# Expert rows without a token skipped, outputs scattered by assignment, all low halves on VectorE

## The reference

```
# hierarchical_moe: 4 groups of 8 experts, top group, then 2 experts inside it; N = 1024 tokens
gate = p_g * softmax(top_v);  expert = g_idx * 8 + top_i          # (N, 2): 2048 assignments
dest_sorted = pstarts[e_sorted] + arange(2N) - starts[e_sorted]   # slots: blocks of 128, one expert each
buf_tok = zeros(P).at[dest_sorted].set(tok_flat[order])           # a slot without a token holds token 0
out_buf = map(lambda tok, e: (silu(xt[tok] @ w1[e]) * (xt[tok] @ w3[e])) @ w2[e], blocks)
y = einsum('nk,nkd->nd', gate, out_buf[dest])
# then x = x + y, and an RMS norm with a gain
```

## Time and profile before

| | us |
|---|---|
| median of 3 runs | 2969.07 |
| profiled execution | 2971.06 |
| its span, first to last instruction | 2969.2 |
| mean granted TensorE clock | 0.947 |

### The profile page before, as it was taken

The page is one execution under the profiler, slowest core; times in us unless marked ns, Lnnn a source line. Parts: engine busy times, 40 slices in busy tenths (PEclk is TensorE's granted clock), DMA queues, the critical chain, the costliest instruction groups (busy, mean ns, idle before and its releaser), DMA issues. The chain is left out here.

```text
span 2969.2 us, 31008 instructions
## 1 busy us (share of the span) xinstructions
PE 2599.6 (88%) x12104; PEld 2095.0 (71%) x12104; DVE 1203.7 (41%) x1637; ACT 1177.7 (40%) x1701; POOL 1036.8 (35%) x613
## 2 busy tenths in 40 slices
PE   6999978879899999899978799938977999999991
PEld 5888856668778878688867577835766777777770
DVE  4530027754122212223436522005135666666654
ACT  3212227754232122123214422214215777777762
POOL 3212203323212122313204532354103667666662
PEclk9999989999999999999979999979987999999995
DMA  4432145532211130422144333371444999999976
GB/s 152 145 119 92 53 102 138 130 93 86 85 50 43 64 107 29 118 75 92 57 136 141 107 121 110 132 289 57 148 186 178 374 375 374 384 374 373 375 293 248
DMA packets 173025, 490.35 MB, mean 165 GB/s; under 512 B 13936, under 2 KB 81552, under 8 KB 160208
## 3 DMA queue, kind: packets, MB, share of 16 engines
q1 hardware_dynamic: 117856, 382.62, 36.4%
q10 hardware_dynamic: 40080, 52.97, 4.9%
q0 software_dynamic: 14944, 52.78, 4.8%
HBM read 389.23 MB, written 99.09 MB: 164 GB/s over the span
## 5 line engine op out<-in xcount | busy, mean ns | idle before, releaser
L2524 ACT ACTIVATE ex_w_hi<-ex_w 128x2048 fp32r<-128x2048 f32 x198 | 378.7, 1916 | 169.8 <-DMA ex_w<-w 102.6
L2584 DVE TENSOR_TENSOR ex_w_lo<-ex_w,ex_w_hi 128x2048 fp32r<-128x2048 f32 x132 | 345.3, 2654 | 197.8 <-ACT ex_w_hi L2524 197.8
L227 POOL TENSOR_TENSOR p_w_lo<-w_raw,p_w_hi 128x512 fp32r<-128x512 f32 (+1 forms) x154 | 198.1, 1316 | 621.5 <-ACT p_w_hi L247 620.1
L2408 POOL TENSOR_TENSOR ex_w_lo<-ex_w,ex_w_hi 128x2048 fp32r<-128x2048 f32 x66 | 340.5, 5183 | 205.2 <-ACT ex_w_hi L2524 205.2
L227 POOL TENSOR_TENSOR p_w_lo_rest<-w_raw,p_w_hi_rest 128x512 fp32r<-128x512 f32 x94 | 123.1, 1343 | 275.0 <-ACT p_w_hi_rest L247 275.0
L366 PE MATMUL o_ps<-o_w_hi,o_m_hi 128*128 128x512 f32 x384 | 154.9, 403 | 19.8 <-POOL split_cols L1028 19.8
L368 PE MATMUL o_ps<-o_w_hi,split_cols 128*128 128x512 f32 x384 | 153.1, 399 | 0.0
L367 PE MATMUL o_ps<-o_w_lo,o_m_hi 128*128 128x512 f32 x384 | 152.9, 398 | 0.0
L366 PE MATMUL ex_pa<-ex_w_hi,ex_xT_hi 128*128 128x512 f32 x264 | 108.2, 410 | 31.4 <-issue 28.7
L1028 POOL TENSOR_TENSOR split_cols<-plain_cols,o_m_hi 128x1024 fp32r<-128x1024 f32 x24 | 57.3, 2391 | 214.0 <-ACT o_m_hi L1078 214.0
L366 PE MATMUL p_ps<-p_w_hi,hT_hi 128*128 128x512 f32 (+1 forms) x320 | 121.6, 380 | 2.6 <-PEq L279 2.6
(11 more groups left out here) (429 smaller groups left out, 6607.2 us busy)
## 6 DMA issues: line engine op xcount, KB each, us to landing
ex_w<-w SPq DMA_DIRECT2D x99, 2048.0 KB, 15.4
w_raw<-w_in SPq DMA_DIRECT2D x42, 1024.0 KB, 5.2
y_slots<-ex_y ACTq DMA_DIRECT2D x33, 512.0 KB, 12.0
y_slots<-xp_zero POOLq DMA_DIRECT2D x32, 512.0 KB, 16.8
att_k<-k_columns SPq DMA_DIRECT2D x48, 256.0 KB, 7.8
x_rows<-o_x SPq DMA_DIRECT2D x24, 512.0 KB, 2.6
w_raw<-w_out SPq DMA_DIRECT2D x8, 1024.0 KB, 9.7
qk_columns<-qk_y ACTq DMA_DIRECT2D x16, 512.0 KB, 2.6
```

Source lines behind the costliest of these rows:

```text
L227: emit(self.lo(n)[:, 0:w], self.half(n // (KC // 2), w)[:, n % (KC // 2), :], self.hi(n)[:, 0:w].bitcast(F32), ALU.subtract).then_inc(self ...
L2408: nc.gpsimd.tensor_tensor(w_lo[:, n % RING, :], raw_half(n), w_hi[:, n % RING, :].bitcast(F32), ALU.subtract).then_inc(down_lo, 1)
L2524: nc.scalar.activation(w_hi[:, n % RING, :], raw_half(n), ACT.Copy).then_inc(hi_done, 1)
L2584: nc.vector.tensor_tensor(w_lo[:, n % RING, :], raw_half(n), w_hi[:, n % RING, :].bitcast(F32), ALU.subtract).then_inc(up_lo, 1)
```

## The change

- The zero fill in `memory_projections` is gone.
- The token table holds, per slot, k x 1024 + token + 1 instead of the token. `slot_row` is that less 1 where it is positive and a row past the end where it is zero; `slot_token` is the token, again past the end where there is none. Gathers have a bounds check that skips such rows. The gather buffer `xg` is cleared once by POOL during `route`, and now outlives that stage. `dest` is gone.
- y of a block is scattered by POOL into `y_rows` (2048 rows: assignment k of token t at k x 1024 + t), skipping empty slots, in place of ScalarE's store of all 128.
- `combine` loads these rows plainly, the first half on SP among the x tiles, the second on ScalarE's queue; its gathers are gone.
- The two low halves of w2 are made by VectorE, in the order of pieces; POOL makes none.

```
 # memory_projections, POOL
                 weights.take_los(pool)
-                nc.gpsimd.memset(zero[:, :], 0.0).then_inc(zero_ready, 1)
-                pool.wait_ge(zero_ready, 1)
-                for b in range(2 * S // P, NBLK):
-                    pool.dma_start(y_slots[b * P:(b + 1) * P, :], zero[:, :]).then_inc(cleared, 16)
-                pool.wait_ge(cleared, 16 * (NBLK - 2 * S // P))
 # route
+            @block.gpsimd
+            def _(pool):
+                nc.gpsimd.memset(xg[:, :, :], 0.0)
-                step(V.tensor_copy(dest[:, :, :], dest_f[:, :, :]))
                 for k in range(2):
-                    ins = V.tensor_tensor(d2[:, k * NT:(k + 1) * NT, :], d2[:, k * NT:(k + 1) * NT, :],
-                                          c.const("tokid").unsqueeze(2).to_broadcast([P, NT, NBLK]), ALU.mult)
+                    half = d2[:, k * NT:(k + 1) * NT, :]
+                    ins = V.scalar_tensor_tensor(half, c.const("tokid").unsqueeze(2).to_broadcast([P, NT, NBLK]),
+                                                 float(k * S + 1), half, ALU.add, ALU.mult)
-                V.memset(slot_token[:, NBLK:], 0)
-                step(V.tensor_copy(slot_token[:, 0:NBLK], pt[:, 0:NBLK]))
+                step(V.tensor_scalar(d2[:, 0, :], pt[:, 0:NBLK], 0.5, float(NOWHERE), ALU.is_lt, ALU.mult))
+                step(V.scalar_tensor_tensor(d2[:, 1, :], pt[:, 0:NBLK], -1.0, d2[:, 0, :], ALU.add, ALU.add))
+                V.tensor_copy(slot_row[:, :], d2[:, 1, :])
+                step(V.tensor_scalar(d2[:, 2, :], d2[:, 1, :], float(S), -float(S), ALU.is_ge, ALU.mult))
+                step(V.tensor_tensor(slot_token[:, :], d2[:, 1, :], d2[:, 2, :], ALU.add))
 # experts, POOL (in gather: bounds_check=S - 1, oob_is_err=False)
-                def take_lo(n):
-                    m, b, half = pieces[n]
-                    pool.wait_ge(hi_done, n + 1)
-                    nc.gpsimd.tensor_tensor(w_lo[:, n % RING, :], raw_half(n), w_hi[:, n % RING, :].bitcast(F32),
-                                            ALU.subtract).then_inc(down_lo, 1)
+                def scatter(b):
+                    pool.wait_ge(y_ready, b + 1)
+                    nc.gpsimd.indirect_dma_start(y_rows, bass.IndirectOffsetOnAxis(slot_row[:, b:b + 1].bitcast(U32), 0),
+                                                 y[:, b % 2, :], None, bounds_check=2 * S - 1, oob_is_err=False
+                                                 ).then_inc(y_out[b % 2], 16)
                 for n, m, b, half in steps():
-                    if n is not None and n + 3 in pieces and pieces[n + 3][0] == "w2":
-                        take_lo(n + 3)
                     if m == "turn_x" and b + 2 < NB:
                         gather(b + 2)
+                    if m == "w1" and half == 1 and b >= 2:
+                        scatter(b - 2)
+                scatter(NB - 2)
+                scatter(NB - 1)
 # experts, ScalarE, in store(b, n)
-                    act.wait_ge(y_ready, b + 1)
-                    act.dma_start(y_b[b], y[:, b % 2, :]).then_inc(y_out[b % 2], 16)
 # experts, VectorE
-                                            ALU.subtract).then_inc(up_lo, 1)
+                                            ALU.subtract).then_inc(down_lo if m == "w2" else up_lo, 1)
-                    if n is not None and n + 3 in pieces and pieces[n + 3][0] != "w2":
+                    if n is not None and n + 3 in pieces:
                         take_lo(n + 3)
 # combine, SP
                     sp.dma_start(x[:, t, :], x_t[t]).then_inc(x_in[t], 16)
+                    sp.dma_start(y[:, t, 0, :], y_rows[t * P:(t + 1) * P, :]).then_inc(y_in[t], 16)
 # combine, POOL
-                for t in range(NT):
-                    for k in range(2):
-                        nc.gpsimd.indirect_dma_start(y[:, t, k, :], None, y_slots,
-                                                     bass.IndirectOffsetOnAxis(dest[:, k, t:t + 1].bitcast(U32), 0)
-                                                     ).then_inc(y_in[t], 16)
 # combine, ScalarE
+                for t in range(NT):
+                    act.dma_start(y[:, t, 1, :], y_rows[S + t * P:S + (t + 1) * P, :]).then_inc(y_in[t], 16)
...
```

More of the change, by code:

```diff
@@ L46 @@
 NBLK = NE + NEXTRA
+NOWHERE = 8 * S
 CONST_COLS = dict(ident=P, ones=P, causal=P, before=P, iota=P, tokid=NT, blk=NBLK, sel=MH * P, iota32=NT * NE,
@@ L1884, in memory_weights, with memory_projections @@
     return Weights(c, stack, "p3", sources, groups, pre=4, first=4)
-def memory_projections(c, weights, hT, q_dram, qT, kT, v, y_slots):
+def memory_projections(c, weights, hT, q_dram, qT, kT, v):
     nc, io = c.nc, c.io
@@ L1897, in memory_projections @@
         mnT = Split(nc, s, "mnT", [P, KC, NMEM])
-        zero = s.enter_context(nc.sbuf_tensor("xp_zero", [P, D], F32))
         qs = s.enter_context(nc.sbuf_tensor("xp_q", [P, NB, BANK], F32))
@@ L1908, in memory_projections @@
         done, freed = weights.done, weights.freed
-        zero_ready, cleared = c.sem("xp_zero_ready"), c.sem("xp_cleared")
         q_out, q_in = [c.sem(f"xp_q_out{b}") for b in range(NB)], c.sem("xp_q_in")
@@ L2114, in load_router, with route @@
     sp.dma_start(bias[:, NG:], io["b_re_2"].partition_broadcast(P)).then_inc(w_in, 16)
-def route(c, expert_weights, pl, bias, gates, dest, slot_token, extra_expert, n_rest):
+def route(c, expert_weights, pl, bias, gates, slot_token, slot_row, extra_expert, n_rest, xg):
     nc = c.nc
@@ L2305, in load, with experts @@
             sp.dma_start(self.w2s[j][:, :], self.w2[at].rearrange("e p n -> (e p) n")).then_inc(self.w2_in[j], 16)
-def experts(c, weights, xn, y_slots, slot_token, n_rest):
+def experts(c, weights, xn, y_rows, slot_token, slot_row, n_rest, xg):
     nc = c.nc
     KF, HALF, RING, NB = FF // P, KC // 2 * FF, 4, NE + 1
-    y_b = y_slots.rearrange("(b p) d -> b p d", p=P)
     def steps():
@@ L2348, in experts @@
         w_hi, w_lo = sb("w_hi", [P, RING, HALF], F32R), sb("w_lo", [P, RING, HALF], F32R)
-        idx, xg = sb("idx", [P, 1], I32), sb("x", [P, 2, D])
+        idx = sb("idx", [P, 2], I32)
         xT_hi, xT_lo = sb("xT_hi", [P, D], F32R), sb("xT_lo", [P, D], F32R)
@@ L2401, in gather @@
                     nc.gpsimd.indirect_dma_start(xg[:, b % 2, :], None, xn,
-                                                 bass.IndirectOffsetOnAxis(slot_token[:, b:b + 1].bitcast(U32), 0)
-                                                 ).then_inc(x_in[b % 2], 16)
-                def take_lo(n):
-                    m, b, half = pieces[n]
-                    pool.wait_ge(hi_done, n + 1)
-                    nc.gpsimd.tensor_tensor(w_lo[:, n % RING, :], raw_half(n), w_hi[:, n % RING, :].bitcast(F32),
-                                            ALU.subtract).then_inc(down_lo, 1)
+                                                 bass.IndirectOffsetOnAxis(slot_token[:, b:b + 1].bitcast(U32), 0),
+                                                 bounds_check=S - 1, oob_is_err=False).then_inc(x_in[b % 2], 16)
+                def scatter(b):
[3 more added lines that the diff above has]
+                                                 ).then_inc(y_out[b % 2], 16)
                 gather(0)
@@ L2414, in _ @@
                 for n, m, b, half in steps():
-                    if n is not None and n + 3 in pieces and pieces[n + 3][0] == "w2":
-                        take_lo(n + 3)
                     if m == "turn_x" and b + 2 < NB:
                         gather(b + 2)
+                    if m == "w1" and half == 1 and b >= 2:
+                        scatter(b - 2)
+                scatter(NB - 2)
+                scatter(NB - 1)
                 def regather(i):
                     pool.wait_ge(r_free, i + 1)
-                    nc.gpsimd.tensor_copy(idx[:, :], slot_token[:, bass.ds(i + NB, 1)]).then_inc(r_idx, 1)
+                    nc.gpsimd.tensor_copy(idx[:, 0:1], slot_token[:, bass.ds(i + NB, 1)])
+                    nc.gpsimd.tensor_copy(idx[:, 1:2], slot_row[:, bass.ds(i + NB, 1)]).then_inc(r_idx, 1)
                     pool.wait_ge(r_idx, i + 1)
@@ L2425, in regather @@
                     nc.gpsimd.indirect_dma_start(xg[:, 0, :], None, xn,
-                                                 bass.IndirectOffsetOnAxis(idx[:, :].bitcast(U32), 0)
-                                                 ).then_inc(r_x_in, 16)
+                                                 bass.IndirectOffsetOnAxis(idx[:, 0:1].bitcast(U32), 0),
+                                                 bounds_check=S - 1, oob_is_err=False).then_inc(r_x_in, 16)
+                    pool.wait_ge(r_y_ready, i + 1)
+                    pool.sem_inc(r_gathers, 1)
+                    nc.gpsimd.indirect_dma_start(y_rows, bass.IndirectOffsetOnAxis(idx[:, 1:2].bitcast(U32), 0),
+                                                 y[:, 0, :], None, bounds_check=2 * S - 1, oob_is_err=False
+                                                 ).then_inc(r_y_out, 16)
```

(30 more changed lines are left out.)

## The result

The changed kernel takes **2879.13 us** (median of 4 runs, 2878.57 to 2883.64) against 2969.32 beside it: ratio **0.9701**, 95% interval 0.9684 to 0.9718.

A forecast was written before the change was run, and what follows sets the result against it. It took the bare zero fill and, in the expert blocks, a loop through POOL's low halves and SP's issue as bounds. Terms -41.1 - 1.5 + 0.6 - 36.0 - 1.7 + 1.5 - 1.0 = -79.2 gave 2890 us, range 2880 to 2908.

The forecast's parts named there:

- Zero fill: End of the memory projections: the fill is bare on the path; without it the next stage starts 41.1 us sooner.
- the clock's term of 1.5: Start of attention after the memory projections: 1.5 us gained, the granted clock no longer being lower there.
- So the bound is this chain, through POOL, not the bytes: Expert blocks: POOL's low halves, SP's issue, w1's landing and VectorE's low half set the 19.55 us period.
- The loop of 39.3 us: Expert blocks: 15.6 to issue, 15.8 landing, 1.9 ScalarE, 4.2 VectorE, 1.85 to TensorE, for two blocks.
- The blocks' floor: Expert blocks: TensorE alone needs 18.30 us per block; with 0.05 for chance waits 18.35, gaining 36.0 over 30.
- Bytes worth nothing: Expert blocks: fewer rows cut DMA work from 18.4 to 17.1 us per block, below 18.30, gaining nothing alone.
- the fullest engine in the chances: Case for the expert blocks: fullest engine or occasional waits, 2893 to 2908 us, chance 0.18.
- VectorE's order: Expert blocks: six low halves fit, 15.9 us per block, at least 3 us slack; SP released at 11.1.
- Scatter: Expert blocks: a POOL scatter costs 3.0 us like a gather (1.0 to 3.0), replacing ScalarE's store, hidden.
- The rival that POOL's indirect transfers shut VectorE out: Expert blocks: VectorE needs 21.9 us per block and becomes the bound, 3003 to 3006 us; slower had chance 0.02.
- End of the experts: Last blocks: 1.7 us saved on waits for POOL's low half and the store; last scatter in the open costs 1.5.
- Final sum: Final stage: plain loads replace sixteen gathers, third tile starts 2 to 3 us sooner; taken as -1.0 (-5 to +3).

The follow-up runs named there:

- e1: Kernel before without its zero fill, all else kept; 2925.04 us, ratio 0.9853.
- e2: Kernel before with VectorE also making both low halves of w2, fill and full transfers kept; 2924.11 us, ratio 0.9848.
- e3: Kernel before with SP asking for the next block's w1 and w3 ahead of this block's w2; 2970.04 us, ratio 1.0003.
- e11: Kernel before with only the second of w2's two low halves moved to VectorE; 2927.45 us, ratio 0.9859.
- e5: Kernel before without zero fill and with all low halves on VectorE, no skipping, scatter or plain loads; 2880.21 us, ratio 0.9700.
- e8: Changed kernel with empty slots not skipped, so all 4224 rows move both ways; 2882.35 us, ratio 0.9703.
- e7: Changed kernel with 2 MB more copied per block and skipped slots spread over all partitions; 2978.05 us, ratio 1.0022.
- e6: Changed kernel with 2 MB more copied per block from DRAM to DRAM on SP's queue; 2996.73 us, ratio 1.0088.
- e9: Changed kernel with two POOL subtractions per block added on a buffer no one reads; 3022.98 us, ratio 1.0178.
- e4: Changed kernel with w2's low halves back on POOL, ahead of its gathers and scatters; 2964.25 us, ratio 0.998.

## Why the prediction was right, and where it was wrong

- **Zero fill: right** in place and size (41.8 for 41.1), and e1 shows it alone. No run shows the clock's term of 1.5 by itself. Shown are 12 score products at 2.83 us for 5.46, with the granted clock at 1.00 for 0.50, and 1.6 less over the whole of attention. That 1.6 fits only this pair of traces: attention took 200.5 in the one before, but 203.1 to 203.3 in the three others that keep the fill (e2, e3, e11), 4.2 to 4.4 over the changed kernel's 198.9, while the wait at the fill was 1.2 to 1.4 shorter in them. That the term came out to 0.1 is luck.
- **"So the bound is this chain, through POOL, not the bytes": POOL right, chain wrong.** The loop of 39.3 us through SP's issue and the landings was a sum that happened to agree with two blocks. w1's landing wasn't what came last: e3 took the wait for it away and gained nothing. The real loop is 19.56 us, on chip, through POOL's two subtractions and VectorE's low half that waits them out. The row with the answer was there: VectorE's 4.17 us. I read it as a slow operation (4.2 in the loop) and never asked when it would have ended had it started earlier. The gain came out nearly right because moving the low halves opens the real loop as well as the one I had in mind, and TensorE is next in both cases; that it did was luck.
- **The blocks' floor was 0.15 too high**, and I added 0.05 for chance waits that don't occur: 30 x (18.35 - 18.147) = 6.1 of the 10.8 us by which the forecast was over. Another 2.0 fell ahead of the change, where the profiled executions differ by up to 10 us, 0.7 at the fill, and 2.5 come from the profiled execution's distance to its median: I took 2.0, it was 4.5. Against them stand 0.8 that the first two blocks lost, which I had not counted; e5 lost none there (45.0).
- **Bytes worth nothing: right** (e2, e5, e8). Not because there was room: with all rows the engines are full at 18.15. My 18.4 us of DMA work per block, the share times the period, overstated it. No run shows the load of a single DMA engine either: the fullest engine in the chances was my estimate. Shown in its place is that e7 was 18.7 us shorter than e6 with the same rows on other partitions, under a DMA bound, and that in e8, with all rows, the blocks stayed at 18.15.
- **VectorE's order: right.** SP at 11.05 for 11.1, low halves of 2.29 in the mean, VectorE 15.9 per block by its window.
- **Scatter: cheaper** than the 3.0 I gave it, 1.01, and the gather too, where it was 2.84 before. What decides is what VectorE does when the transfer starts. In the changed kernel all scatters and 28 of 33 gathers start while VectorE is idle or at a short operation, and take 1.0. A transfer that starts beside a VectorE low half ends 0.8 to 0.9 us after it: 2.84 before, 2.88 for both in e9.
- **The rival that POOL's indirect transfers shut VectorE out** had the right mechanism in the wrong operation. With subtractions on POOL it happens, and e9 is the slower kernel that this rival described. A low half that starts while a transfer is under way still takes 2.28 to 2.29 (19 of them in e2, e5 and e11), so between these two it is the transfer that waits.
- **End of the experts** (0.5 for 0.2): near, but both of its terms were too small. The low halves on VectorE saved 2.8 (e2, 39.9 for 42.8) where I had 1.7, and with the scatter in place of the store the stage is 2.4 longer (42.3 for e5's 39.9) where I had 1.5. **Final sum** (0.9 for 1.0): near. The first tile's wait of 10.87 us for its rows is now what the stage begins with.

## What to carry to other kernels

A loop whose links add up to the period is a candidate and no more: change one link alone (here SP's order) before believing it. An operation that takes twice its usual time (4.17 us for 2.29 here) may be a wait drawn as work; look at what ended one usual duration before it did. And two engines that shut one another out must be costed together: POOL's free time is not free where VectorE is near the critical loop (e9: 22.30 us per block instead of 18.15, for results that no one uses).

## What the runs showed of the hardware

- In e3 and e4 a POOL subtraction of 128x2048 holds up VectorE's low half of the same size wholly: 6.56 and 7.17 us in the two timelines instead of 2.29, and each of the 31 in either trace that ends behind one does so 2.14 to 2.16 us behind it. One that was already running when POOL began wasn't stretched (three in 6.68 in e3, POOL starting within the third); POOL's subtraction then took 5.9 us instead of 4.6. A low half of e4 drawn as begun at 2534.23, during a scatter, ended behind POOL's next subtraction (2534.62 to 2539.24) too. So it is with 9 low halves of e4, drawn as begun 0.2 to 0.7 us before the subtraction, and with 25 of e9 (0.4), each behind a scatter.
- Skipping costs POOL nothing: scatter and gather 1.0 us each with half of the indices out of bounds, and 1.0 in e8 where every row moves, when VectorE is idle at their start. The mean of 1.3 in e8 (72.48 us for 55 of them) comes from those that started beside a low half. A skipped row still leaves a small packet: from 2250 to 2750 POOL's queue has 7944 packets (14.79 MB) in the changed kernel and 7957 (28.93 MB) in e8, and under 512 B there are 5664 packets against e8's 2223; the kernel before has 2036 in as long a stretch.
- DMA engines at share 1.00 still hid entirely under TensorE: in e8 the 30 distances between w1 starts are 18.14 to 18.15 us, as in the changed kernel.
